# A hybrid attention and state-space layer on one core: the work ahead of the split products reordered, and the imaginary state inputs multiplied from a moved copy of u

## What is computed

```python
def hybrid_layer(x, cache_k, cache_v, h0_re, h0_im, p):
    z = rmsnorm(x, p['attn_norm_g']) @ p['w_in']
    q, k, v, u = split_projection(z)
    q = rmsnorm(q, p['q_norm_g']);  k = rmsnorm(k, p['k_norm_g'])
    attn, new_k, new_v = window_attention(q, k, v, cache_k, cache_v, slopes, sinks)
    A_bar = exp(A * dt);  B_bar = ((A_bar - 1) / A) * B          # complex, 64 groups x 64 states
    bu = einsum('ntgh,gph->ntgp', u, B_bar)                      # state inputs, real and imaginary
    h = scan(h[t] = A_bar * h[t-1] + bu[t])
    y_ssm = real(einsum('ntgp,ghp->ntgh', h, C)) + D_skip * u
    g = gelu(y_ssm)
    ssm_out = g * sigmoid(g @ p['w_glu'] + p['b_glu'])
    mix = concatenate([rmsnorm(attn, p['attn_out_g']), rmsnorm(ssm_out, p['ssm_out_g'])])
    h = x + mix @ p['w_out']
    return h + square(relu(rmsnorm(h, p['mlp_norm_g']) @ p['w_mlp_up'])) @ p['w_mlp_down']
```

## Time and profile before

| | us |
|---|---|
| median of 3 runs (1255.35 to 1256.86) | 1255.66 |
| the profiled execution | 1255.49 |
| its span, first to last instruction | 1253.4 |
| PE busy / weight loads busy | 1205.3 (96%) / 1128.4 (90%) |
| DVE / ACT / POOL busy | 721.3 / 412.1 / 152.9 |

### The profile page before, as it was taken

One profiled execution on the slowest core, in us unless ns is written; L12 is line 12 of the kernel. 1 busy time (PEld: TensorE's weight loads), 2 busy tenths in 40 slices (PEclk: granted clock), 3 DMA queues, 4 the chain that ended last, 5 costly groups with the idle time before them and its releaser, 6 DMA issues.

```text
span 1253.4 us, 20187 instructions
## 1 busy us (share of the span) xinstructions
PE 1205.3 (96%) x8478; PEld 1128.4 (90%) x8478; DVE 721.3 (58%) x718; ACT 412.1 (33%) x493; POOL 152.9 (12%) x92
## 2 busy tenths in 40 slices
PE   7999968898999998999999999999999999999997
PEld 5677646577999998999999999999999999999997
DVE  8678679674656554554445544455555544555443
ACT  5000012364445433333333333333333333333331
POOL 2331341000000000010001100010001100010001
PEclk9999998997999999999999999999999999999999
DMA  7333222235444544545554445545544454545552
GB/s 264 134 105 134 68 67 72 107 135 144 150 163 142 186 167 137 167 156 180 168 167 153 160 160 168 168 152 161 182 166 157 159 172 166 168 152 166 181 164 103
DMA packets 54329, 190.33 MB, mean 152 GB/s; under 512 B 7768, under 2 KB 9304, under 8 KB 53848
## 3 DMA queue, kind: packets, MB, share of 16 engines
q1 hardware_dynamic: 54248, 189.09, 45.5%
HBM read 185.82 MB, written 5.28 MB: 152 GB/s over the span
## 4 chain that ended last, share of the span: by engine, by line
PE 92%; DVE 3%; issue 2%; ACT 1%; POOL 0%; POOLq 0%; DMA 0%; ACTq 0%; DVEq 0%
PE psum L1220 92%; DVE states L822 1%; PE psum L1341 0%; DVE q_t L661 0%; DVE r_b L786 0%; DVE states L661 0%; DVE mov_b L1044 0%; ACT gate L549 0%; POOL states L1146 0%; POOL h_t L1146 0%; POOLq L115 0%; DVE w_lo L652 0%; ACT w_hi L419 0%; DMA small<-in_small 0%; ACT pt_head L532 0%
## 5 line engine op out<-in xcount | busy, mean ns | idle before, releaser
L652 DVE TENSOR_TENSOR w_lo<-w_raw,w_hi 128x1024 fp32r<-128x1024 f32 x288 | 401.8, 1405 | 420.8 <-ACT w_hi L419 420.2
L1220 PE MATMUL psum<-mov_b,w_hi 128*128 128x288 f32 x2560 | 511.4, 296 | 6.0 <-issue 4.1
L419 ACT ACTIVATE w_hi<-w_raw 128x1024 fp32r<-128x1024 f32 x288 | 302.7, 1058 | 504.5 <-PE psum L1220 504.5
L1220 PEld LDWEIGHTS psum<-mov_b,w_hi 128*128 128x128 f32 x2560 | 411.8, 189 | 6.9 <-issue 4.7
L1220 PE MATMUL psum<-mov_a,w_hi 128*128 128x288 f32 x2048 | 407.6, 295 | 3.2 <-DVE s_relu L1098 3.2
L1220 PE MATMUL psum<-mov_b,w_lo 128*128 128x288 f32 x1280 | 377.2, 295 | 0.0
L1220 PEld LDWEIGHTS psum<-mov_a,w_hi 128*128 128x128 f32 x2048 | 328.7, 189 | 3.7 <-DVE s_relu L1098 3.7
L1220 PE MATMUL psum<-mov_a,w_lo 128*128 128x288 f32 x1024 | 301.2, 294 | 0.0
L1220 PEld LDWEIGHTS psum<-mov_b,w_lo 128*128 128x128 f32 x1280 | 243.0, 190 | 0.0
L1220 PEld LDWEIGHTS psum<-mov_a,w_lo 128*128 128x128 f32 x1024 | 193.9, 189 | 0.0
L1220 PE MATMUL psum<-x_g,w_raw 128*128 128x288 f32 x640 | 167.9, 421 | 20.6 <-DVE q_t L661 13.3
(11 more groups left out here) (165 smaller groups left out, 514.8 us busy)
## 6 DMA issues: line engine op xcount, KB each, us to landing
w_raw<-in_w SPq DMA_DIRECT2D x336, 512.0 KB, 3.5
h_t<-in_x SPq DMA_DIRECT2D x4, 576.0 KB, 6.8
out_y<-h_t SPq DMA_DIRECT2D x4, 576.0 KB
b_w<-in_b SPq DMA_DIRECT2D x1, 1024.0 KB, 5.5
c_w<-in_c SPq DMA_DIRECT2D x1, 1024.0 KB, 7.9
k_cache<-in_kc SPq DMA_DIRECT2D x1, 1024.0 KB, 5.6
v_cache<-in_vc SPq DMA_DIRECT2D x1, 1024.0 KB, 5.7
out_kc<-in_kc SPq DMA_DIRECT2D x1, 992.0 KB
```

Source lines behind the costliest of these rows:

```text
L419: nc.scalar.activation(hi3[:, n % SLOTS, :], raw3[:, n % SLOTS, :], ACT.Copy) \
L652: nc.vector.tensor_tensor(lo3[:, n % SLOTS, :], raw3[:, n % SLOTS, :], hi3[:, n % SLOTS, :].bitcast(F32), ALU.subtract) \
L1220: return nc.tensor.matmul(out, lhs_t, rhs, start=start, stop=stop)
```

## The change

- VectorE folds the squares of x right after the rotation tables, ahead of the discretisation; PE sums them after 10 of the 16 k-tiles of `g_u0`.
- For the pairs j >= 4 the imaginary matmul reads a copy of u that lies 64 partitions away (`au`, written by ACT with `move_u`, two copies of 64x288 for each k-tile, 14 copies in all), and the imaginary B of those pairs is laid out in the same way on the host. Its rows are then 32*((j+2) % 4).
- The products with C are placed among the last k-tiles of `g_kv` and the first two of `g_q0`; `turn_out(0, 2)` comes ahead of the eviction of `g_kv`. Eight tiles of `g_q0` still lie between the sets of `bu1`, and six (before: two) behind them.
- The eviction of `g_q0` follows the third chunk of the scan, not the fourth; that of `g_q1` comes ahead of `y_out(1)`. `g_q1` is cut at other tiles.
- At the end of attention the units are renumbered (`pt2`, `pt3` and `pv1` now have the odd banks), `rms_s` is summed in bank 3 of its unit, `spv` waits for `pv0` only, the third transposes come straight ahead of `spv`, and the splits of the first four weight steps of w_out are spread: two ahead of the gate's second half, one in the middle, one behind the attention's root.

```diff
-     ("pt1", 1), ("none", 0), ("sc3", 1), ("none", 0), ("spt", 2), ("none", 0), ("pv0", 1), ("none", 0),
-     ("pt2", 1), ("rms_s", 1), ("spv", 1), ("none", 0), ("pt3", 1), ("none", 0), ("pv1", 1), ("wo0", 1),
-     ("rms_a", 1), ("none", 0), ("wo1", 1), ("wo2", 1), ("wo3", 1), ("up0", 1), ("up1", 1), ("rms_h", 1),
+     ("pt1", 1), ("none", 0), ("sc3", 1), ("none", 0), ("spt", 2), ("none", 0), ("pv0", 1), ("pt2", 1),
+     ("rms_s", 1), ("pt3", 1), ("spv", 1), ("pv1", 1), ("wo0", 1), ("rms_a", 1), ("none", 0), ("wo1", 1),
...
# ACT
+            def move_u(half, q):
+                src, dst = u3[:, 4 * half + q, :], au3[:, q, :]
+                nc.scalar.activation(dst[64:128, :], src[0:64, :], ACT.Copy)
+                nc.scalar.activation(dst[0:64, :], src[64:128, :], ACT.Copy).then_inc(u_moved, 1)
+            for q in range(1, 4):
+                part_read(act, UNIT["g_u0"], q)
+                move_u(0, q)
...
+            unit_read(act, UNIT["g_u1"])
+            for q in range(4):
+                move_u(1, q)
...
             sample_pt_out()
+            hi_part(S_WO)
+            hi_part(S_WO + 1)
             gate_out(1)
             ssm_squares(1)
             pt_out(2)
-            root(r_s, UNIT["rms_s"], 0.25 / SSM_WIDTH)
-            hi_part(S_WO)
+            root(r_s, UNIT["rms_s"], 0.25 / SSM_WIDTH, bank=3)
             pt_out(3)
-            mix_his(gate3, "g_ssm", 0)
+            hi_part(S_WO + 2)
+            mix_his(gate3, "g_ssm", 0, range(4))
             attention_squares(0)
-            hi_part(S_WO + 1)
+            mix_his(gate3, "g_ssm", 0, range(4, QT))
             attention_squares(1)
-            hi_parts(range(S_WO + 2, S_WO + SLOTS))
             root(r_b, UNIT["rms_a"], 1.0 / ATTN_WIDTH)
+            hi_part(S_WO + 3)
             mix_his(q3, "g_attn", QT)
# DVE
             turn_out(0, 1)
+            turn_out(0, 2)
             project_out("g_kv", kv3)
-            turn_out(0, 2)
             turn_out(0, 3)
...
-            scan(1, range(4))
+            scan(1, range(3))
             project_out("g_q0", q3[:, 0:4, :])
-            scan(1, range(4, 6))
+            scan(1, range(3, 6))
...
+            project_out("g_q1", q3[:, 4:8, :])
             y_out(1)
-            project_out("g_q1", q3[:, 4:8, :])
# PE
             def project_pair(half, n):
                 u, j = UNIT[f"bu{half}"], HALF_PAIRS * half + n
+                moved = j >= 4
                 if n % 4 == 0:
                     part_read(pe, UNIT["g_u0"], n // 4) if half == 0 else unit_read(pe, UNIT["g_u1"])
+                    if moved:
+                        pe.wait_ge(u_moved, j // 4)
...
-                rows = slice(32 * (j % 4), 32 * (j % 4) + 32)
                 for r in range(2):
-                    done = mm(psum[:, 4 * (u % 2) + 2 * (n % 2) + r, 0:TOK], bw4[rows, r, j // 4, :],
-                              u3[rows, j // 4, :])
+                    at = 32 * ((j + 2) % 4) if moved and r else 32 * (j % 4)
+                    rows = slice(at, at + 32)
+                    src = au3[rows, n // 4, :] if moved and r else u3[rows, j // 4, :]
+                    done = mm(psum[:, 4 * (u % 2) + 2 * (n % 2) + r, 0:TOK], bw4[rows, r, j // 4, :], src)
...
-            gemm_full("g_kv", S_KV, GROUP_STEPS, xg3)
+            gemm_full("g_kv", S_KV, GROUP_STEPS, xg3, part=range(12))
             project_states(0, 0)
+            gemm_full("g_kv", S_KV, GROUP_STEPS, xg3, part=range(12, 14))
             project_states(0, 1)
-            gemm_full("g_q0", S_Q0, GROUP_STEPS, xg3, part=range(3))
+            gemm_full("g_kv", S_KV, GROUP_STEPS, xg3, part=range(14, KT))
             project_states(0, 2)
-            gemm_full("g_q0", S_Q0, GROUP_STEPS, xg3, part=range(3, 6))
+            gemm_full("g_q0", S_Q0, GROUP_STEPS, xg3, part=range(2))
             project_states(0, 3)
...
-            sum_squares(UNIT["rms_s"], (au3, sq3), ssm_squared)
+            sum_squares(UNIT["rms_s"], 3, (au3, sq3), ssm_squared)
+            turn_probs(3, 5)
             u = UNIT["spv"]
-            unit_free(pe, u)
+            unit_read(pe, UNIT["pv0"])
...
-            turn_probs(3, 5)
             attend(1)
-            gemm(UNIT["wo0"], S_WO, GROUP_STEPS, b4, ready=tiles_ready(mix_lo), part=range(3))
-            sum_squares(UNIT["rms_a"], (au3, sqa3), attn_squared)
-            gemm(UNIT["wo0"], S_WO, GROUP_STEPS, b4, ready=tiles_ready(mix_lo), part=range(3, KT))
+            gemm(UNIT["wo0"], S_WO, GROUP_STEPS, b4, ready=tiles_ready(mix_lo), part=range(4))
+            sum_squares(UNIT["rms_a"], 0, (au3, sqa3), attn_squared)
+            gemm(UNIT["wo0"], S_WO, GROUP_STEPS, b4, ready=tiles_ready(mix_lo), part=range(4, KT))
```

More of the change, by code:

```diff
@@ L562, in attention_squares, with mix_his @@
                 nc.scalar.activation((au3, sqa3)[g], q3[:, 4 * g:4 * g + 4, :], ACT.Square).then_inc(attn_squared, 1)
-            def mix_his(src, name, first):
-                for k in range(QT):
+            def mix_his(src, name, first, tiles=range(QT)):
+                for k in tiles:
                     if k % 4 == 0:
@@ L728, in _, with fold @@
             dve.wait_ge(cos_sin_ready, 1)
+            def fold(tiles, total, first, signal):
+                link(tt(tiles[:, 0:2, :], tiles[:, 0:2, :], tiles[:, 2:4, :], ALU.add))
+                linked()
+                if first:
+                    tt(total[:, :], tiles[:, 0, :], tiles[:, 1, :], ALU.add).then_inc(signal, 1)
+                    return
+                link(tt(tiles[:, 0, :], tiles[:, 0, :], tiles[:, 1, :], ALU.add))
+                linked()
+                tt(total[:, :], total[:, :], tiles[:, 0, :], ALU.add).then_inc(signal, 1)
+            for k in range(4):
+                dve.wait_ge(x_squared, k + 1)
+                if k:
+                    dve.wait_ge(x_summed, k)
+                fold(xsq3[:, 4 * k:4 * k + 4, :], ssq, k == 0, x_summed)
             link(nc.vector.tensor_scalar(am1, abr, -1.0, None, ALU.add))
@@ L1036, in mix_scale, with mix_los @@
                 tt(part, part, over_tiles(buf[:, :], 4), ALU.mult).then_inc(mix_scaled, 1)
-            def mix_los(src, name, first):
-                for k in range(QT):
+            def mix_los(src, name, first, tiles=range(QT)):
+                for k in tiles:
                     dve.wait_ge(mix_hi, first + k + 1)
@@ L1051, in _ @@
             soft_scale(3, 5)
+            lo_part(S_WO)
+            lo_part(S_WO + 1)
             gate_mul(1)
             prompt_out(0)
+            one_over_root(UNIT["rms_s"], r_s)
+            mix_scale(gate3[:, 0:4, :], r_s)
+            mix_scale(gate3[:, 4:8, :], r_s)
             samples_out()
-            one_over_root(UNIT["rms_s"], r_s)
-            for m in range(2):
-                mix_scale(gate3[:, 4 * m:4 * m + 4, :], r_s)
-            lo_part(S_WO)
-            mix_los(gate3, "g_ssm", 0)
+            mix_los(gate3, "g_ssm", 0, range(5))
             prompt_out(1)
-            lo_parts(range(S_WO + 1, S_WO + SLOTS))
+            mix_los(gate3, "g_ssm", 0, range(5, QT))
+            lo_part(S_WO + 2)
             one_over_root(UNIT["rms_a"], r_b)
-            for m in range(2):
-                mix_scale(q3[:, 4 * m:4 * m + 4, :], r_b)
+            mix_scale(q3[:, 0:4, :], r_b)
+            mix_scale(q3[:, 4:8, :], r_b)
+            lo_part(S_WO + 3)
             mix_los(q3, "g_attn", QT)
@@ L1311, in sum_squares @@
                     for k in range(4):
-                        done = mm(banks(unit, 1)[:, 0, :], ones, part[:, k, :], start=m == 0 and k == 0,
+                        done = mm(banks(unit)[:, bank, :], ones, part[:, k, :], start=m == 0 and k == 0,
                                   stop=m == 1 and k == 3)
@@ L1383, in _ @@
                 project_pair(1, 2 * m + 1)
-                gemm_full("g_q0", S_Q0, GROUP_STEPS, xg3, part=range(6 + m, 7 + m))
-            gemm_full("g_q0", S_Q0, GROUP_STEPS, xg3, part=range(14, KT))
+                gemm_full("g_q0", S_Q0, GROUP_STEPS, xg3, part=range(2 + m, 3 + m))
+            gemm_full("g_q0", S_Q0, GROUP_STEPS, xg3, part=range(10, KT))
             pe.wait_ge(const_loaded, 16)
```

39 lines of the change are left out of this document (14 added, 25 removed), and 1 row of the table UNITS.

## The result

| | before | changed |
|---|---|---|
| median of the runs beside each other, us | 1255.51 (4 runs, 1254.05 to 1256.86) | 1228.44 (4 runs, 1225.99 to 1229.08) |
| ratio | 1 | 0.9775, 95% interval 0.9752 to 0.9797 |
| profiled execution / its span | 1255.49 / 1253.4 | 1225.99 / 1223.8 |
| PE busy | 1205.3 | 1190.4 (97%) |

The forecast was 1228.0 us, with a range of 1223.5 to 1234.5. A second set of five runs of the changed kernel gave 1226.55 (first experiment), so the gain is 27 to 29 us. The helpers of before have moved: the matmul's line 1220 is 1240, DVE's tensor-tensor line 661 is 678, the low part's line 652 is 669.

The account below looks back on a forecast made before the run. PE, busy 1205 of 1253 us, was taken as the bound, so only its own time and waits, chiefly 13.3 us for q's first half, could count. Terms totalling -27.5 us on 1255.49 gave 1228.0 us, range 1223.5 to 1234.5.

Parts of the forecast that it names:

- start: Folds and rms_x: folds ahead of the discretisation let the first pair start at 42.05 us instead of 44.49, -2.4 us.
- clock behind it: Less slow clock after a shorter wait: -1.6 us behind the first pair, -0.9 us behind the wait for q's first half.
- sets of half 0: Six moved sets overlap across row groups, two sets taking 6.6 to 6.7 us instead of 7.45: -1.9 us.
- products, order: Products with C and tiles reordered: earlier scan and more breaks between tiles and products cost together +0.7 us.
- sets of half 1: Eight moved sets: first pair to the tile behind the last takes 24.25 us instead of 27.6, -3.4 us.
- wait for q: PE's wait for the eviction of q's first half falls from 13.3 to 2.6 us: -10.7 us.
- q's second half at the scores: Its eviction, now ahead of y_out(1), is done at 212.4 us, before PE comes at 215.7: -2.0 us.
- end of attention and clock in it: From third transposes to PE's last gap -4.3 us; clock fall moving from dense work into new w_lo waits -1.0 us.
- Rival 1: In the pairs' sets, moved copies do not let the two matmuls overlap; gain 22.5 us, 1233 us; chance 10%.
- Rival 2: End of attention gives nothing back: low clock into wo0 and a longer chain eat the rest; 1233.3 us; chance 14%.
- Rival 3: DVE later than walked, at the start or third scan chunk: 2 to 3 us more waiting for q; 1231; 9%.
- rival 4: Clock stands at 1.2 GHz through both stretches of sets and the tiles behind them: slower, 1272 us; chance 3%.

Follow-up runs that it names:

- first experiment: The changed kernel measured again with no edit, five runs and a second profile (also called the repeat): median 1226.55 us, ratio to before 0.9765.
- one split: Changed kernel with w_out's fourth weight step split ahead of the root and reciprocal of rms_a: median 1227.48 us, ratio to before 0.9793.

## Why the prediction was right

Its steps, against the first profile of the changed kernel (us; minus is gained):

| step | forecast | profile |
|---|---|---|
| start | -2.4 | -1.9 |
| clock behind it | -1.6 | -1.6 |
| sets of half 0 | -1.9 | -2.2 |
| products, order | +0.7 | +0.9 |
| sets of half 1 | -3.4 | -3.4 |
| wait for q | -10.7 | -10.9 |
| clock behind it | -0.9 | -2.5 |
| q's second half at the scores | -2.0 | -2.0 |
| end of attention and clock in it | -4.3 and -1.0 | -4.9, -0.7 behind the gap |
| **sum** | **-27.5** | **-29.6** by the spans |

The steps' rows follow one another (44.49 to 42.60; 72.95 to 67.30; 142.65 to 130.06; 154.25; 172.12; 213.87), each less what was gained before it, and they leave 0.4 us of rounding by the scores.

- **Start.** The folds took 10.2 us (17.02 to 27.21), not 7.2: GpSimd worked beside them from 18.71 to 25.1. Those 3 us are more than the named cover of 1.8, but the discretisation then took 9.1 us instead of 13.3, which the forecast had not counted on, so that the reciprocal ended at 38.3, ahead of the forecast 39.6. Here two errors cancelled. The pair was 0.55 us later than forecast because the tiles ahead of it ran slower at the very start (22.66 us for the first ten k-tiles); in the repeat it started at 41.19. The forecast of 42.05 lies between.
- **Sets.** A free set took 0.72 us where 0.85 was estimated, two sets 6.49 where 6.6 to 6.7 were. DVE held back every second set, as said, and still idled 0.9 us in two. Rival 1 (no overlap) was refuted by the rows and by the kernel with copies in the same rows. The prediction read the Trainium skill too narrowly here: that matmuls start and end in program order (TensorE: Matmul & The Clock Gate, Part 3) does not forbid that they run at once, and the same part says that matmuls in different row groups do, with a speedup of 3.07 for four of 32 rows and 512 columns. The rows, of 288 columns in float32, agree with that: the four start within 0.04 us, and the set takes 0.72 us where four of full height take 1.95, a factor of 2.7. What stands in the prediction as the skill's case against the change was no such case.
- **Wait for q.** Forecast 2.6 us, measured 2.4; DVE done at 172.0 as forecast, after the samples' addition at 159.23 (159.1) and the third chunk at 170.74 (170.7). The undone parts show how it is made up: 5.6 us with the fourth chunk ahead, 10.1 with the old products.
- **Clock.** This is where a size was off. A short fall behind q's wait, 1.6 us, was forecast; there was none in the first profile, and one that cost 1.7 us (0.66 over 5 us) in the repeat. So the term was right for one execution of the kernel and wrong for another. The fall in the samples' product came, without idling, as forecast.
- **End of attention.** Forecast -4.3, measured -4.9 between scores and gap; the kernel with the old end, +4.0, shows that it is this edit that gives it. `w_lo` waits of 3.2 and 1.1 us were forecast as 3.2 and 1.4. The clock's fall at 333 us went, as forecast (1.5 us where 1.0 was taken). It moved into the wait for `w_lo` in the repeat, but not in the first profile. Rival 2 is refuted by the same kernel.
- Rival 3 (DVE late) and rival 4 (the clock low through the sets) have no row for them: DVE came at the forecast times, and PEclk is 1.00 over 44 to 68 and over 130 to 154 us.
- **Luck.** That the forecast of 1228.0 lies within half a microsecond of the median 1228.44 is partly chance. It is 2.0 us above the profile whose steps stand here and 1.5 above the median of the second set of runs, and the errors of the terms have both signs (+0.5 at the start, -1.6 at the clock).

The parts undone one at a time cost 5.95, 3.6, 3.8, 6.7 and 4.0 us, 24 us together, of the 27 to 29. One step was not undone by itself: the eviction of q's second half ahead of `y_out(1)`, 2.0 us by the rows. With it the sum is 26. What is left is within the error of five differences; whether the parts also cover for each other was not tested.

## What to carry to other kernels

When an engine's wait ends with another engine's chain, move independent work into the wait (four tiles here, 6.7 us) and take work out of that chain (one chunk of the scan, 3.8 us). Speeding up the waiting engine ahead of the wait is not lost if it also paces that chain: the faster sets gave 6 us, with the wait as long as before. The next bound should be walked forward before the move, since here 2.4 us of wait removed brought the scores only 1.1 us forward. After a reordering, look where the engines that feed the bound idle just ahead of a new wait: three weight splits moved into 7 to 8 us of idling of ACT and DVE gave 4.4 to 5.8 us by the profiles, no less than the whole new end of attention (4.0). A partial cure that moves a wait and leaves its length may show nothing (one split: 0.9 us at the gap, none in the median).

## What the runs showed of the hardware

- Four float32 matmuls of 32 rows in four row groups run side by side: 0.72 us for the set, 1.24 us (before) and 1.21 us (no copies) in two row groups; a single one of full height takes 0.488 us. The first passes of all four start between 49.95 and 49.99 us, the second ones between 50.29 and 50.34.
- ACT moved 64x288 values by 64 partitions in 0.44 us a copy, as long as a copy in the same partitions takes, and without any cost that the medians show.
- Beside GpSimd's work DVE's folds took 10.2 us instead of 7.2, without idling between them; the discretisation took 13.3 us beside it and 9.1 without. The order of the two changed their sum by 1.2 us only (20.5 to 19.3).
- The clock fell to 1.2 GHz with PE busy throughout, in matmuls of 16 columns, and stayed at 2.4 GHz behind a wait of 2.4 us in one execution and fell in another of the same kernel; the same holds for the wait of 3.2 us for `w_lo`. The nine runs of the changed kernel lie between 1224.85 and 1229.08 us, 2 us either way.
